# Mixture-of-experts stage with 160 slots per expert, shared blocks of four experts and one extra block, where there were 192 slots and shared blocks of two

## What is computed

```python
scores = sigmoid(xt @ router_w); sel = scores + router_bias
grp_score = top_k(sel.reshape(T, 4, 4), 2)[0].sum(-1)
best = argmax(grp_score)                     # one group per token
_, idx = top_k(where(in_best_group, sel, -inf), 2)
gate = scores[idx] / scores[idx].sum()
hb = silu(xb @ w_gate[e]) * (xb @ w_up[e]);  yb = hb @ w_down[e]     # per expert
y = (yb * gate).sum over the token's two experts
x = layer_norm(ALPHA * x + y)
```

## Times and profile of the kernel before

| | us |
|---|---|
| median of 3 runs | 2425.74 |
| lowest and highest | 2425.72, 2426.42 |
| profiled execution | 2424.13 |
| its span, first to last instruction | 2422.8 |
| stage of experts, from the first projection | 2118.2 |
| second expert's projection | 2133.8 |
| last matmul's end | 2406.9 |

### The profile page before, as it was taken

How to read it: one execution, slowest core, us unless ns; L and a number is a source line. 1 busy time by engine, 2 the same in 40 slices (tenths; PEclk the granted TensorE clock), 3 DMA queues, 4 the chain that set the end, 5 groups by cost and what they waited for, 6 DMA issues and landing times.

```text
span 2422.8 us, 25957 instructions
## 1 busy us (share of the span) xinstructions
PE 2330.7 (96%) x9707; PEld 1360.6 (56%) x9707; DVE 1275.2 (53%) x2620; ACT 588.2 (24%) x1349; POOL 661.0 (27%) x543
## 2 busy tenths in 40 slices
PE   8899999999999999999999999999999999699995
PEld 4676657764444444444444676654464554387883
DVE  4544425454567778777663556666611346611226
ACT  2344433331132221232221211111100221111125
POOL 1000000044543444443272000006541036212124
PEclk9999999999999999999999999999999999799998
DMA  7000210122110110110224400003160213648885
GB/s 235 1 1 18 70 36 1 48 82 73 35 35 18 35 35 18 36 35 18 96 63 141 115 9 14 35 35 131 61 228 33 70 46 126 211 126 238 260 275 191
DMA packets 151740, 201.86 MB, mean 83 GB/s; under 512 B 18984, under 2 KB 109992, under 8 KB 151608
## 3 DMA queue, kind: packets, MB, share of 16 engines
q1 hardware_dynamic: 142536, 180.45, 22.5%
q0 software_dynamic: 8208, 19.46, 3.3%
q10 hardware_dynamic: 864, 0.22, 0.0%
HBM read 171.20 MB, written 39.34 MB: 87 GB/s over the span
## 4 chain that ended last, share of the span: by engine, by line
PE 88%; DVE 4%; POOL 3%; issue 2%; DMA 2%; ACT 1%; SPq 0%; POOLq 0%; ACTq 0%; DVEq 0%
PE banks L171 81%; PE banks L174 6%; DMA x_scratch<-arena,places 1%; DMA arena<-x_scratch 1%; POOL arena L1473 1%; POOL arena L1491 0%; DVE arena L930 0%; POOL arena L1468 0%; POOL arena L259 0%; POOL arena L1474 0%; DVE arena L2074 0%; POOL arena L1476 0%; DVE arena L469 0%; DMA arena<-x_scratch,slots 0%; DVE arena L3587 0%
## 5 line engine op out<-in xcount | busy, mean ns | idle before, releaser
L171 PE MATMUL banks<-arena 128*128 128x512 f32 (+16 forms) x8131 | 2182.1, 457 | 51.4 <-DVE arena L3604 11.3
L171 PEld LDWEIGHTS banks<-arena 128*128 128x128 f32 (+6 forms) x8131 | 1195.6, 183 | 940.6 <-issue 837.4
L174 PE MATMUL banks<-arena 128*128 128x128 f32 (+1 forms) x1480 | 210.0, 277 | 23.8 <-DMA arena<-x_scratch,slots 6.9
L174 PEld LDWEIGHTS banks<-arena 128*128 128x128 f32 (+1 forms) x1480 | 169.8, 141 | 91.9 <-issue 68.0
L2204 POOL TENSOR_TENSOR arena<-arena 128x512 f32<-128x512 f32 (+3 forms) x160 | 154.5, 967 | 166.6 <-ACT arena L2015 146.9
L259 POOL TENSOR_TENSOR arena<-arena 128x1 f32<-128x1 f32 (+1 forms) x94 | 75.9, 808 | 454.1 <-DVE arena L2740 311.8
L1468 POOL TENSOR_TENSOR arena<-arena 128x512 f32<-128x512 f32 x4 | 9.3, 2320 | 573.0 <-PE banks L174 453.4
L2015 ACT ACTIVATE arena<-arena 128x512 f32<-128x512 f32 (+4 forms) x160 | 81.6, 575 | 314.3 <-DVE arena L2106 313.1
L2074 DVE TENSOR_TENSOR arena<-arena 128x512 f32<-128x512 f32 (+3 forms) x160 | 106.6, 726 | 28.4 <-ACT arena L2007 28.3
L2106 DVE TENSOR_TENSOR arena<-arena,banks 128x512 f32<-128x512 f32 (+4 forms) x160 | 89.6, 628 | 1.1 <-PE banks L174 1.1
L2058 DVE SCALAR_TENSOR_TENSOR arena<-banks,arena 128x512 f32<-128x512 f32 (+3 forms) x128 | 61.5, 541 | 34.3 <-PE banks L171 34.3
(11 more groups left out here) (349 smaller groups left out, 1791.0 us busy)
## 6 DMA issues: line engine op xcount, KB each, us to landing
x_scratch<-arena SPq DMA_DIRECT2D x40, 512.0 KB, 2.9
arena<-in_o_w_in_dram SPq DMA_DIRECT2D x32, 512.0 KB, 5.5
arena<-x_scratch SPq DMA_DIRECT2D x32, 512.0 KB, 6.0
arena<-in_w_gate_dram SPq DMA_DIRECT2D x16, 1024.0 KB, 12.0
arena<-in_w_up_dram SPq DMA_DIRECT2D x16, 1024.0 KB, 15.3
arena<-in_w_down_dram SPq DMA_DIRECT2D x16, 1024.0 KB, 8.1
arena<-in_x_dram SPq DMA_DIRECT2D x16, 512.0 KB, 7.4
arena<-in_w_in_dram SPq DMA_DIRECT2D x16, 512.0 KB, 7.2
```

Source lines behind the costliest of these rows:

```text
L171: return pe.matmul(o, a, b, start=start, stop=stop)
L174: return pe.transpose(o, a, ident)
```

## The change

An expert keeps 128 slots of its own and gets 32 in a block that four experts of four different groups share (160 in all). ORDER now goes through the groups: 0, 4, 8, 12, then 1, 5, 9, 13 and so on. Between the second and the third four stands one item more, MORE, with a block of 128 slots for the rows over 160 of the one expert that has them. Its weights are loaded from the address that a register gives, and the register is read from the second word of the flag. So there are 17 items and 21 blocks. The flag's first word is 1 if two experts have over 160 rows, or one over 288.

```diff
-LIMIT = 192
-NS = 192
-ORDER = tuple(8 * a + 4 * side + c for a in range(2) for c in range(4) for side in range(2))
+LIMIT = 160
+MOST = 288
+NS = 160
+MORE = 20
+ITEMS = 17
+ORDER = (0, 4, 8, 12, 1, 5, 9, 13, MORE, 2, 6, 10, 14, 3, 7, 11, 15)
...
-        WD = [scr(24, 2048), scr(32, 2048)]
+        WD = [scr(24, 2048), scr(32, 2048)] + [A[:, 2048 * i:2048 * i + 2048] for i in range(3)]
...
+        def one_expert(w, e):
+
+            if ORDER[e] < MORE:
+                return w[0][ORDER[e]].rearrange("(k p) c -> p k c", p=128)
+            if which[0] is None:
+                Y.wait_ge(flag_done, 1)
+                which[0] = sync.value_load(FLG[0:1, 1:2], min_val=0, max_val=15)
+            return w[0][bass.ds(which[0], 1)].rearrange("a (k p) c -> p (a k) c", p=128)
...
-        HTs = [scr(43 + 1.5 * i, 2 * NS) for i in range(3)]
+        HTs = [scr(45 + 2.5 * i, 2 * NS) for i in range(4)] + [A[:, 7424 + 320 * i:7744 + 320 * i] for i in range(2)]
...
+        QUAD = [0] * 4 + [1] * 4 + [None] + [2] * 4 + [3] * 4
+        FIRST = [0, 4, 9, 13]
...
+        ROWS = 5
+        PUTS = len(DOWN) - ROWS
...
         def units_at(x, place):
-            return {(13, "turned"): (0, 1), (14, "gated"): (3,), (14, "turned"): (4,), (15, "gated"): (7,)}.get((x, place), ())
+            return {(15, "gated"): (0, 1), (15, "turned"): (2, 3), (16, "gated"): (4, 5), (16, "turned"): (6, 7)}.get((x, place), ())
 
         def units_behind(i):
-            return {18: (2,), 19: (5,), 20: (6,)}.get(i, ())
+            return {PUTS + 2: (8,), PUTS + 3: (9, 10)}.get(i, ())
...
         def pool_put(i):
             c = column(i)
             G.wait_ge(ys_a, i + 1)
             G.wait_ge(ys_v, i + 1)
-            G.wait_ge(d_put, 48 * (i // 3))
+            for b in range(3):
+                G.wait_ge(d_put[b], puts_of(b, puts_in_front(i)))
...
+            for r in range(ROWS):
+                pool_unit_rows(r)
+            for u in range(NT + 1):
                 pool_unit_root(u)
...
         def sp_moe():
             meet(Y, out4_over)
             for d, n in x4_stored:
                 Y.wait_ge(d, n)
+            Y.wait_ge(r_done, NT)
+            for x in range(2, 5):
+                load_down(x)
             load(XB[0], row(ln_moe_g_2[0]), d_g)
             load(XB[1], row(ln_moe_b_2[0]), d_g)
-            for x in range(1, 13):
-                Y.wait_ge(gu_done, x)
-                load_expert(x + 3)
-                Y.wait_ge(dn_done, 3 * ((x - 1) // 2 + 1))
-                load_down(x + 1)
-            Y.wait_ge(d_put, 288)
+            for x in range(1, ITEMS):
+                if x + 3 < ITEMS:
+                    Y.wait_ge(gu_done, x)
+                    load_expert(x + 3)
+                if x >= 5:
+                    Y.wait_ge(gu_done, min(x, 14))
+                    Y.wait_ge(dn_done, last_down(x - 5))
+                    load_down(x)
+            all_put(Y)
+            Y.wait_ge(gu_done, 14)
             for t in range(5):
                 load_unit(t)
...
+                else:
+                    for n in range(2):
+                        for k in range(2):
+                            for q in range(4):
+                                y = FIRST[DOWN[i][1]] + q
+                                m = mm(bank((2, 6)[i % 2] + n)[32 * q:32 * q + 32, :],
+                                       HTs[y % 6][:, NS * k + 128:NS * k + 160],
+                                       tiled(WD[y % 5], 2)[:, k, 512 * n:512 * n + 512], k == 0, k == 1)
```

More of the change, by code:

```diff
@@ L212, in program @@
         w_o4 = [tiled(weights("out 4a", 3, 1), 8), tiled(weights("out 4b", 1, 1), 8)]
-        wgu = [tiled(weights(f"expert {e}", turns[e % 4], 2), 8) for e in range(16)]
+        wgu = [tiled(weights(f"expert {e}", turns[e % 4], 2), 8) for e in range(ITEMS)]
         c_v = event("vector_step")
@@ L3541, in program @@
         d_out = d_wa.again()
-        for d_ in d_xg:
-            d_.block(96)
-        d_base = [d.again() for d in d_xg] + [event(f"last_rows_landed_{i}") for i in range(2)]
-        FREE = [[WR[turns[i]][:, 1024 * k:1024 * k + 1024] for k in range(4)] for i in range(3)]
+        for j_, d_ in enumerate(d_xg):
+            d_.block(16 * len([j for j in range(len(TURNED)) if j % 4 == j_]))
+        d_base = [d.again() for d in d_xg] + [event("last_rows_landed")]
+        FREE = [[WR[turns[i]][:, 1024 * k:1024 * k + 1024] for k in range(4)] for i in (1, 2)]
         def unit(u):
@@ L3775, in moe_turned @@
         def moe_turned(eng, copy, j, k0, src, done):
[L3776 to L3785 removed]
+            kind, x = TURNED[j]
+            if kind == "s":
+                for q in range(4):
+                    y = FIRST[x] + q
+                    eng.wait_ge(gu_done, y - 5)
+                    if y % 6 > 3:
+                        eng.wait_ge(gs_done, 1)
+                    m = copy(XT[y % 6][:, k0:k0 + 4, 128:160], tiled(src, 4)[:, :, 32 * q:32 * q + 32])
+            else:
+                eng.wait_ge(gu_done, x - 5)
+                if x % 6 > 3:
+                    eng.wait_ge(gs_done, 1)
+                m = copy(XT[x % 6][:, k0:k0 + 4, 0:128], tiled(src, 4))
             m.then_inc(done.sem, 1)
@@ L3813, in act_moe @@
                     act_unit(u)
-                for j in moe_turns(x):
+                for j in turns_in(x):
                     act_moe_turned(j)
@@ L3827, in act_moe @@
                         act_unit(u)
-            for u in range(NT, UNITS):
+            for u in range(NT + 3, UNITS):
                 act_unit(u)
@@ L3839, in dve_moe @@
             dve_slot_gates()
-            for x in range(17):
-                if x < 16:
+            for x in range(ITEMS + 1):
+                if x < ITEMS:
                     ge = GEX[x % 2]
@@ L3908, in pe_all @@
         def pe_all():
+            P.wait_ge(fb_x4, 16)
+            P.wait_ge(ys_a, PUTS)
+            P.wait_ge(ys_v, len(DOWN))
+            for t in range(NT):
+                P.wait_ge(fb_ta, t)
+                P.wait_ge(fb_tv, t)
+                turn_tile(OTf[t], fb_turned)
+            P.wait_ge(fb_ta, NT)
+            P.wait_ge(fb_tv, NT)
             for e in range(16):
@@ L3935, in act_all @@
         def act_all():
+            for t in range(NT):
+                C.wait_ge(fb_turned, 2 * t + 1)
+                act.activation(HT[:, 0:4, 128 * t:128 * t + 128], tiled(bank(4), 4), ACT.Copy).then_inc(fb_ta.sem, 1)
             for i in range(128):
@@ L3957, in dve_all @@
             V.wait_ge(fb_x4, 16)
+            for t in range(NT):
+                V.wait_ge(fb_turned, 2 * t + 2)
+                vec.tensor_copy(HT[:, 4:8, 128 * t:128 * t + 128], tiled(bank(5), 4)).then_inc(fb_tv.sem, 1)
             for i in range(128):
@@ L4108, in constants @@
     import numpy as np
-    c = np.zeros((128, C_N + 128), np.float32)
-    c[:, C_N:] = np.arange(128)[None, :]
+    c = np.zeros((128, C_N + 160), np.float32)
+    c[:, C_N:C_N + 128] = np.arange(128)[None, :]
+    for e in range(16):
+        shared = 128 * (16 + e % 4) + 32 * (e // 4) - 128
+        c[:, C_N + 128 + e] = shared - 128 * e
+        c[:, C_N + 144 + e] = 128 * MORE - LIMIT - shared
     c[:, C_ID:C_ID + 128] = np.eye(128)
```

346 lines of the change are left out of this document (158 added, 188 removed).

## The result

| | before | after |
|---|---|---|
| median, us | 2425.72 (5 runs, 2422.90 to 2426.42) | 2387.19 (5 runs, 2386.16 to 2388.24) |
| ratio | | 0.9844, 95% interval 0.9833 to 0.9855 |
| span of the profiled execution, us | 2422.8 | 2384.9 |

The kernel is 1.6% faster: 2387.19 us where 2388 was forecast, and a span of 2384.9 where 2384.7 was.

The account below looks back on a forecast made before the run. PE, busy 96% of the span, was taken to bound the kernel. PE's -33.2 us, the head's +2.6 and about 6 given back by the tail brought the span to 2384.7, forecast as 2388 us, range 2379 to 2401.

Parts of the forecast that it names:

- PE's sum: Stage of experts: projections -19.0 us, shared blocks -15.0, turns -2.6, one more down projection +3.4, in all -33.2 us.
- The head: Start of the expert stage: first gathers land later beside three downs moved ahead, +2.3, small copies +0.3: +2.6 us.
- The tail's start: Last put lands 7.2 us after issue, at 2325.4; ACT first uses a tile 9.7 us later, at 2335.1.
- Rival 1: Tail: row loads come late and hold up ACT, DVE and PE one for one, 2394 to 2401 us; chance 0.16.
- The tail's pace: Tail: ACT needs 2.51 and DVE 2.45 us per tile; last 8 tiles and 3 row additions take 23.7 us.
- The end: End of the span: 3.4 us after DVE's last output, as before, so at 2384.7.
- The 11.34 us of the earlier trace: Tail: PE's 11.34 us wait behind DVE's row addition goes, since row gathers are issued right behind the put.
- (2): Head and tail: tail hidden better and first gathers not delayed, 2379 us; chance 0.10.
- (3): Shared blocks: 32-row records run two by two or with loads on top, +12 to +14, 2400 to 2402 us; chance 0.05.
- (4): Middle of the stage: DMA sets the pace, no item below 16.2 us, 2390 to 2400 us; chance 0.05.
- (5): The branch computing every expert for all tokens is taken, at least 1320 us more, over 3700; chance 0.02.
- (6): Extra item with the register's address brings nothing, or shared slots stay idle: no change, 2421 to 2430 us; chance 0.02.

Follow-up runs that it names:

- e1: Kernel after, with the down weights of the third to fifth expert asked for only behind the first turns, norm rows ahead of them: 2382.54 us.
- e10: e8 plus the gate and up weights of the third and fourth item asked for behind the first turned blocks too: 2382.95 us.
- e2: Kernel after, with the down weights of the last two items asked for behind the first five tile loads of the tail: 2386.11 us.
- e9: Edits of e2 and e8, plus tile 0 normed by ACT and DVE behind the turn of item 14: 2380.12 us.
- e8: e1 plus DVE's first addition of gathered rows moved behind its copy of item 15's turned block: 2382.16 us.
- e5: Kernel before, with gate and up projections over 160 of 192 slot columns and nothing else changed: 2402.74 us.
- e4: Kernel after, with the two inner loops of a shared block's down projection exchanged, expert outside and parts inside: 2387.52 us.
- e6: Kernel after, with half of every gate and up projection left out, all loads, turns, downs, puts and gathers kept: 2346.38 us (one run).
- e3: Kernel after, with the extra item's weights loaded from a constant address in place of one read from the flag: 2386.29 us.

## Why the prediction was right, point by point

| step | predicted | measured |
|---|---|---|
| record of 160 columns | 137 ns | 135.8 |
| record of 128 columns in the extra item | 111 ns | 111.6 |
| shared block of four | 3.8 us | 3.77 |
| first projection starts | 2120.8 | 2121.42 |
| second projection starts | 2134.8 | 2135.15 |
| last block put into memory is through PE | 2317.1 | 2316.68 |
| its put has landed | 2325.4 | 2327.7 |
| ACT starts on tile 0 | 2335.1 | 2334.59 |
| DVE's second step of item 15 and its copy end | near 2344 | 2343.5 |
| PE's loss before item 16's projection | about 1 | 0.97 |
| DVE's second step of item 16 ends | 2357.5 | 2356.66 |
| DVE's last output ends | 2381.2 | 2379.65 |
| end of the span | 2384.7 | 2384.9 |

**PE's sum.** It stood on two prices, the line between 128 and 192 columns and the 32-row record read 60 us ahead of the stage. Both held to 1%. The stage from the second projection to the last put took 181.5 us where 182.3 were summed.

**The head** was mis-sized. The gathers' delay was taken as 2.3 us, the step from the first gather to the median of all; e1 shows that it is 3.5. Three small things took back most of the difference: the indices, put at 0, were ready 0.43 us sooner (2106.73 against 2107.16); the four small copies cost 0.13 us (1.07 us of idle time of PE ahead of the first projection against 0.94), where 0.3 was forecast; and the first projection with what stands behind it took 13.73 us where the forecast had 14.0. The bound was chosen well (0 to 4.7) and the value in it by a wrong likeness: the median gather ran beside a DMA share of 0.8, and the new first gathers ran beside 1.03 to 1.05.

**The rule on the queues.** The Trainium skill (DMA: Bandwidth & Descriptors, Issuing engines are not separate DMA queues) says that DMAs of all issuers share 16 engines, and e1 agrees: loads that SP issued held up gathers that POOL issued. e10 adds a limit: up to a share of 0.78 the sharing cost nothing (4.72 us at 0.78, 4.71 at 0.00).

**The tail's start** came out right for a wrong reason. The steps were put landed, 7.2 us; then 9.7 us until ACT has the first tile. The put took 9.45 us, 2.3 more than the median, beside three downs asked for at 2316.71; e2 shows 1.8 us of that to be theirs. The step that failed is "from the first such load to ACT's first use it took 9.7 us, so 2335.1 here". Before, ACT did wait for the tile (3.75 us), which came behind 4 MB of weights that SP had asked for in the 8 us ahead of it, at a DMA share of 1.04 from 2342 to 2347 and 1.08 in the 5 us behind. Now the last weights are asked for 11 us ahead, the first tile was there at most 6.9 us after its load (2327.71 to 2334.59, no wait), and in e9 after 3.2. So ACT no longer waits for it: what starts the tail is the tanh of item 15, behind PE's gate half (2334.25). The 2.3 us too few and the 2.8 or more too many cancelled. Rival 1 rested on the same step: e2 moved the landing by 1.8 us, and the end stayed. A stretch of the kernel before, just ahead of its tile loads, and one of e9, ahead of its own, show the two queues:

```profile
2342.00:2347.00 5.00, 5.00 (x33) 5.00 (x32) 0.56 (x1) 0.49 (x1) 1.91 (x2) 1.00 1.04 368
```

```profile
2320.00:2323.00 3.00, 3.00 (x25) 3.00 (x25) 0.32 (x1) 0.00 (x0) 0.00 (x0) 1.00 0.13 27
```

**The tail's pace** was right: ACT's and DVE's passes, one after the other. The forecast of the tail lacked one wait, DVE's 9.79 us for the first row gather, which landed after 8.3 us where the quickest took 3.7 before; by e8 it was worth some 0.9 us at most. The 8 tiles and 3 row additions took 23.0 us, where 23.7 were summed.

**The end** came 5.25 us after DVE's last output instead of 3.4. The last put was issued 1.2 us after that output's end in both (2420.59 before, 2380.85 after); the rest is its landing. Before, the last block held no row at all, since experts 11 and 15 have 105 and 91 rows; now the last shared block holds the rows of four experts over 128, 11 and 29 of them. The puts of this line took 2.2 to 4.4 us to land before and 3.4 to 4.5 after. That the empty block is the reason fits, but no run varied it.

**The 11.34 us of the earlier trace rows** are gone, as forecast: PE's idle times in the tail are 0.97, 0.62 and 2.51 us. e5, which keeps the old order of the tail, still has such a stall of 10.53 us.

**The rivals.** No delay in the head and a better hidden tail (2), priced at 2379: not in the kernel after, but e9, which has both, comes to 2380.12. The shared block near 7 us, or with its loads on top (3): refuted by 3.77 us, and by e4 in the other order. DMA sets the pace (4): refuted, but not by much. The prediction put DMA's pace at 16.2 us per item if the share of 0.81 was near the limit; e6 measures 12.0. The share of 0.98 between 2192 and 2249 shows how little cover is left. The fallback branch (5) wasn't taken; its margin before was 13 tokens and not the 12 of the prediction, since the flag asks for over 192 rows and the fullest expert has 180. The address by a register (6) costs nothing (e3).

## What to carry to other kernels

Price a new shape on a full engine from its nearest neighbours in the trace, and take the same form's record from anywhere in the program: this forecast the 182 us from the second projection to the last block put into memory to within 1 us. Before a transfer is moved ahead of a gather that an engine waits for, read the DMA share at that point: at 0.8 there was room at no cost, and above 1.0 the first projection came 3.5 us later. And a landing time from the trace of before holds only with the queue that stood ahead of it there: the first tile took 9.7 us behind 4 MB of weights and 3.2 us with the DMA share at 0.13.

## What was not expected of the hardware

**The clock's rise in the head.** The 80 records of the first projection took 9.67 (e4), 11.26, 11.31 (the kernel after), 11.36, 11.89, 11.93, 11.99, 11.99 and 12.01 us in nine kernels that have the same 80. In the stretch around their start:

```profile
2120.00:2125.00 5.00, 3.93 (x30) 3.72 (x29) 3.57 (x12) 0.79 (x4) 1.40 (x2) 1.00 0.59 190
```

is e4 with a granted clock of 1.00, which is 2.4 GHz, and

```profile
2120.00:2125.00 5.00, 3.93 (x16) 3.56 (x15) 3.57 (x12) 0.75 (x4) 1.31 (x2) 0.50 0.64 221
```

is e2, at the lower level of 1.2 GHz, with PE busy for the same 3.93 us. The moment at which TensorE goes from 1.2 to 2.4 GHz there is worth up to 2.3 us between these profiles, of which there is one for each kernel. PE stood idle for 6.8 to 10.1 us ahead of the first turn in all of them, behind the gather. What sets the moment wasn't tried and stays open; part of the spread within e4's 2384.49 to 2389.14 may be this.

**Gathers beside loads.** The row gathers of the tail landed in 3.7 to 5.5 us before, and in 8.3 to 13.9 us beside the 4 MB of tiles and the downs. The DMA engines gave up to 411 GB/s in the head (share 1.03), where most of it was weights; with gathers, puts and weights mixed (e6) they stayed at 334 GB/s at a share of 1.05.
